# Hybrid attention and linear-recurrence block on one core: the seven-product output from token tile 2 on, weights' sums moved to VectorE in two rounds, the residual's loads moved

## The chip, the cores and the metric

One core of a Trainium2 chip. The metric is the device time in microseconds of one execution. TensorE (PE) multiplies, VectorE (DVE), ScalarE (ACT) and GpSimd (POOL) work elementwise, SyncE (SP) issues nearly all DMAs; ACT issues the stores of the result.

## The reference, cut to what matters

```python
h = rmsnorm(x, w_norm_pre)                      # x: 2048 x 1024, fp32
proj = h @ w_in                                 # 1024 x 3328
q_a, k_a, v_a, z_a, q_r, f_r, i_r, z_r = split(proj)
o_a = sliding_window_sink_attention(rope(q_a), rope(k_a), v_a, sinks) * silu(z_a)   # 8 heads of 64, chunks of 64, window 128
o_r = rmsnorm(hgrn2_chunkwise(q_r, f_r, i_r, lb), hgrn_norm) * silu(z_r)            # 4 heads of 128, a state carried along the sequence
y = concatenate([o_a, o_r]) @ w_out             # 1024 x 1024
x = x + rmsnorm(y, w_norm_post)
```

## The kernel before, in words

The sequence is cut into four token tiles (TILES, index t) of N = 512 tokens. All matmuls of the projections take fp32 operands split in two parts, a rounded one (hi) and the rest (lo); a product is hi x hi + hi x lo + lo x hi, so three matmuls for each block of 128 input features.

In each token tile PE first computes 26 products of the projection (w = 0 to 25: K, V, four tiles of Q, four of the attention's gate Z, then for each of the four recurrent heads forget, query, value and gate), 24 matmuls of 512 columns each, in `products` (line 566). Between them `between` places the small matmuls of attention (scores, transposes of the probabilities, their product with the values) and of the recurrence at fixed places (w, m). Then comes the output product. In token tile 0 it is plain (`out_plain`): eight weight tiles (OUT0 to OUT0 + 7), 192 matmuls (line 575) into eight PSUM banks. In token tiles 1 to 3 (t >= FAST, FAST = 1) it is done with seven products of half-sized blocks instead of eight (`out_fast`, line 822): four weight tiles of w_out as they are (B11, B21, B12, B22) and four sums of them (T1 to T4), against mixes that are also sums (s3, S1, S2, S4). It has 14 weight tiles P1A to P3B of 1 MB (hi and lo), each used by 12 matmuls, 168 in all, in the order UNITS.

Each engine runs its own queue in program order. The other engines go through steps s = 0 to 33 of a token tile; in step s they treat mainly product s - 1. DVE's steps 2 to 7 hold the turns of rope (`rope_turn`, lines 1288 to 1299), 7 to 10 the gates, 8 to 15 the softmax of four pairs of chunks (`softmax_first`, `softmax_sums`), 11 to 26 the heads' gates and scans, and after each head's output `gate_head`, `mix_head` and, in tiles with seven products, `sum_head`, which makes S2, S1 and S4 of the head. The queue's order is written out by hand.

Weights come through SP. In tile 0, and for the first six of tile 1 (index below FRESH), a raw tile of 0.5 MB is loaded into one of four slots of w_raw, ACT makes its hi part (`split_hi`), DVE its lo part (`split_lo`, line 1230), and SP saves both to DRAM (`save_split`); later tiles load the saved pair (`load_split`, line 449: 0.5 MB hi, 0.5 MB lo) into one of four slots of w_hi and w_lo. A slot is loaded when the product that used it last is done (`wait_slot`) and its save has landed (`wait_saved`, line 362). In each round of the loop over w, SP first may load a raw tile, then save, then load a pair, then issue loads of x for the next token tile (`load_x` at w = H0 + 0, 2, 4, 6), and so on; what stands first holds the rest.

T1 to T4 are made in tile 1, in two rounds (SUMS_AT = steps 5 and 11): SP loads the four quarters of w_out raw (`load_sums`, at w = 6 and 13), POOL forms four differences in w_raw (line 1653), ACT the four hi parts in mix_hi and mix_lo (`sums_high`, line 982), POOL the four lo parts (line 1658), SP saves all (`save_sums`, lines 467 and 468, at w = 11 and 18).

At the end of a token tile the output is scaled by the post norm's weights (`post`, L1425), its squares are summed on ACT (`square_fast`), and the result is y * scale + residual (`finish_y`, L1430, one DVE instruction for each 128x512 block; two of the eight blocks go to POOL in two instructions, L1706 and L1708). The residual is loaded into x_in by two DMAs of 1 MB (`load_residual`, line 485). In tiles with seven products they are issued after the loads of P3A and of P3B. After the last final, DVE makes the low part of the next tile's sum of squares (`x_low`, L1481), which PE wants before product 2 (`sum_x`).

Of the kernel before, what the change touches and what calls it, by code (L numbers as in the profile page):

```python
# [30 lines left out]
P = 128  # L31
# [30 lines left out]
FAST = 1  # L62
# [6 lines left out]
SPLIT_SLOT = SPLIT_SLOT + [w % 4 for w in range(FAST_WT)] * (TILES - FAST)  # L69
assert WT == 34 and OUT0 == 26 and FAST_WT % 4 == 0 and FAST == 1  # L70
# [8 lines left out]
def index(t, w):  # L79
    return w if t == 0 else WT + (t - FAST) * FAST_WT + w  # L80


def where(i):
    return (0, i) if i < WT else (FAST + (i - WT) // FAST_WT, (i - WT) % FAST_WT)
# [84 lines left out]
class Count:  # L169
# [4 lines left out]
    def __init__(self, sem, per_tile, first=None):  # L174
        self.sem, self.per_tile, self.first = sem, per_tile, per_tile if first is None else first
# [4 lines left out]
    def after(self, tile, i):  # L180

        assert -(self.first or self.per_tile if tile == 1 else self.per_tile) <= i < (self.per_tile if tile else self.first)
        return self.per_tile + (self.first + (tile - 1) * self.per_tile if tile else 0) + i + 1


def hybrid_block(nc, x, x_rows, weights, cos, sin, vectors, w_post, squares, out, kept):
# [3 lines left out]
    with ctx:  # L190
# [138 lines left out]
        y_read, y_biased, finished = count("y_read", 8), count("y_biased", 1), count("finished", 8 - len(Y_POOL))  # L329
# [545 lines left out]
        def _(act):  # L875
# [133 lines left out]
            for t in range(TILES):  # L1009
                links[0] = 0  # L1010
                for s in range(WT):
# [72 lines left out]
                    if t == FAST:  # L1084
                        for j, first in enumerate(SUMS_AT):
                            for k in (0, 1) if s == first + 2 else (2, 3) if s == first + 3 else ():
                                sums_high(4 * j + k)
# [682 lines left out]
```

## Time and profile before

| | us |
|---|---|
| median of three runs | 906.81 (905.63 to 908.21) |
| profiled execution | 907.85 |
| its span, first to last instruction | 906.0 |
| PE busy | 862.3 (95%) |
| DVE, ACT, POOL busy | 655.3, 525.8, 167.9 |

The profile is of one execution. Times in its views are microseconds from the span's start; what is added to the span for the execution's time is 1.85 us. PE is busy as long as a matmul is under way; since matmuls are pipelined, one of 512 columns is shown with 0.39 us while the next starts 0.227 us after it. SPq is SP's DMA issue. The clock is the one granted to TensorE as a share of 2.4 GHz.

### The profile page before, as it was taken

To read this page: it belongs to the slowest core of one execution; us is meant where nothing else is said; L and a number is where in the kernel's file an instruction comes from. 1 tells how busy PE (TensorE), PEld (TensorE's weight loads), DVE (VectorE), ACT (ScalarE), POOL (GpSimd) and SP (SyncE) were. 2 spreads that over 40 slices of the span, in tenths; PEclk is the share of its full clock that TensorE was granted. 3 is DMA by queue.
4 is the path that set the end of the run, shared out by engine and by line. 5 is a ranking of instruction groups with operands and counts; after the bars stand their busy time and mean duration, and the time that the engine had idled before them with its cause. 6 is when DMAs were issued, how large, how long until landed. Compare 5 with 4: busy or idle time off the path is not lost.

```text
span 906.0 us, 12482 instructions
## 1 busy us (share of the span) xinstructions
PE 862.3 (95%) x4406; PEld 703.4 (78%) x4406; DVE 655.3 (72%) x1127; ACT 525.8 (58%) x1041; POOL 167.9 (19%) x109
## 2 busy tenths in 40 slices
PE   7999999999998987999979999999989999999994
PEld 6887888888876776887868877888868887888883
DVE  6778868773775798889654579998755368987835
ACT  7666456563565457666535555865833755667533
POOL 0000014320244062252120000144202000013112
PEclk9999999999998998999999999999999999999998
DMA  8685755649877957455897554454789544443677
GB/s 308 219 308 193 280 209 181 231 154 410 349 254 289 392 228 298 169 181 192 300 377 289 205 193 163 140 183 166 277 331 367 197 174 146 166 153 143 226 282 279
DMA packets 61709, 217.49 MB, mean 240 GB/s; under 512 B 6864, under 2 KB 7120, under 8 KB 61648
## 3 DMA queue, kind: packets, MB, share of 16 engines
q1 hardware_dynamic: 58912, 209.75, 63.4%
q10 hardware_dynamic: 2736, 6.95, 1.9%
q8 instruction: 35, 0.57, 0.2%
q14 instruction: 26, 0.21, 0.1%
HBM read 164.25 MB, written 52.43 MB: 239 GB/s over the span
## 4 chain that ended last, share of the span: by engine, by line
PE 57%; DVE 20%; DMA 10%; ACT 5%; issue 4%; SPq 3%; POOL 1%; DVEq 0%; ACTq 0%
PE bank L566 41%; DMA w_lo<-kept_lo 4%; PE bank L822 3%; DVE kv_tok L1352 3%; DMA kept_lo<-w_lo 3%; PE turn_b L822 3%; PE score_b L822 2%; PE score_b L599 2%; ACT probs_t L923 1%; DVE q_gate L1430 1%; PE turn_b L623 1%; DMA x_in<-in_x_rows 1%; PE turn_b L676 1%; PE turn_b L679 1%; DVE f_c L1594 1%
## 5 line engine op out<-in xcount | busy, mean ns | idle before, releaser
L566 PE MATMUL bank<-h_hi,w_hi 128*128 128x512 f32 x832 | 326.5, 393 | 6.5 <-DMA w_lo<-kept_lo 4.8
L566 PE MATMUL bank<-h_hi,w_lo 128*128 128x512 f32 x832 | 329.0, 395 | 0.0
L566 PE MATMUL bank<-h_lo,w_hi 128*128 128x512 f32 x832 | 327.5, 394 | 0.0
L566 PEld LDWEIGHTS bank<-h_hi,w_hi 128*128 128x128 f32 x832 | 157.5, 189 | 40.7 <-DMA w_lo<-kept_lo 6.4
L566 PEld LDWEIGHTS bank<-h_lo,w_hi 128*128 128x128 f32 x832 | 157.3, 189 | 35.1 <-issue 3.3
L566 PEld LDWEIGHTS bank<-h_hi,w_lo 128*128 128x128 f32 x832 | 157.3, 189 | 33.2 <-issue 0.5
L1673 POOL TENSOR_TENSOR mix_lo<-v_r,mix_hi 128x512 fp32r<-128x512 f32 x16 | 21.2, 1325 | 424.1 <-ACT v_r L1111 424.1
L1230 DVE TENSOR_TENSOR w_lo<-w_raw,w_hi 128x1024 fp32r<-128x1024 f32 x37 | 45.8, 1248 | 33.4 <-ACT w_hi L896 32.9
L1352 DVE STREAM_TRANSPOSE kv_tok<-k_mid 32x128 f32<-32x128 f32 x192 | 58.1, 303 | 2.8
L896 ACT ACTIVATE w_hi<-w_raw 128x1024 fp32r<-128x1024 f32 x38 | 39.7, 1050 | 22.4 <-DMA kept_lo<-w_lo 9.0
L911 ACT ACTIVATE g_a<-g_a 128x512 f32<-128x512 f32 x32 | 20.2, 632 | 47.0 <-DVE g_a L1310 47.0
L900 ACT ACTIVATE g_a<-g_b 128x512 f32<-128x512 f32 x32 | 20.1, 629 | 44.3 <-DVE g_b L1306 44.3
L1643 POOL TENSOR_TENSOR x_acc<-x_acc,x_sq 128x512 f32<-128x512 f32 x21 | 30.0, 1427 | 75.7 <-ACT x_sq L946 75.7
L1430 DVE SCALAR_TENSOR_TENSOR q_gate<-q_gate,y_stats,x_in 128x512 f32<-128x512 f32 x24 | 27.3, 1172 | 18.4 <-DMA x_in<-in_x_rows 17.6
L1310 DVE SCALAR_TENSOR_TENSOR g_a<-g_b,g_a 128x512 f32<-128x512 f32 x32 | 24.9, 779 | 17.8 <-ACT g_a L902 17.8
L1036 ACT ACTIVATE f_b<-bank 32x512 f32<-32x512 f32 x48 | 28.3, 589 | 15.8 <-PE bank L566 15.2
L932 ACT ACTIVATE kv_tok<-f_d 32x128 f32<-32x128 f32 x96 | 29.5, 307 | 7.0 <-DVE f_d L1534 6.0
L1706 POOL TENSOR_TENSOR q_gate<-q_gate,y_stats 128x512 f32<-128x512 f32 x8 | 10.1, 1264 | 113.8 <-DMA x_in<-in_x_rows 81.4
L1653 POOL TENSOR_TENSOR w_raw<-w_raw 128x1024 f32<-128x1024 f32 x8 | 21.0, 2632 | 50.5 <-DMA w_raw<-in_weights 50.2
L932 ACT ACTIVATE probs<-f_d 32x128 f32<-32x128 f32 x96 | 29.5, 307 | 1.2
L1594 DVE TENSOR_TENSOR_SCAN f_c<-reset,f_b 128x512 f32<-128x512 f32 x16 | 19.6, 1225 | 11.5 <-ACT f_b L1094 11.5
L822 PE MATMUL score_b<-w_hi,s_hi 128*128 128x512 f32 x36 | 15.2, 423 | 12.7 <-DMA w_lo<-kept_lo 12.7
(265 smaller groups left out, 1657.6 us busy)
## 6 DMA issues: line engine op xcount, KB each, us to landing
w_hi<-kept_hi SPq DMA_DIRECT2D x114, 512.0 KB, 3.7
w_lo<-kept_lo SPq DMA_DIRECT2D x114, 512.0 KB, 4.7
w_raw<-in_weights SPq DMA_DIRECT2D x46, 512.0 KB, 5.8
kept_hi<-w_hi SPq DMA_DIRECT2D x34, 512.0 KB, 6.3
kept_lo<-w_lo SPq DMA_DIRECT2D x34, 512.0 KB, 7.2
x_in<-in_x_rows SPq DMA_DIRECT2D x8, 1024.0 KB, 10.3
x_in<-in_x SPq DMA_DIRECT2D x15, 512.0 KB, 6.7
out<-q_gate ACTq DMA_DIRECT2D x9, 512.0 KB, 7.9
```

The source lines that it names most:

```text
L566: mm = pe.matmul(acc(w)[:, :], stationary[:, s, k, :], moving[:, k, :], start=(m == 0), stop=(m == 3 * KT - 1), skip_group_check=True)
L822: mm = pe.matmul(into, mix, weight, start=w in (P1A, P7A, P2A, P4A) and k == 0 and part == 0, stop=k == KT // 2 - 1 and part == 2, skip_gr ...
L896: act.activation(w_hi[:, SPLIT_SLOT[i], :, :], w_raw[:, i % RAW_SLOTS, :, :], ACT.Copy).then_inc(hi_split.sem, 1)
L932: copy = act.activation(square(v_tok(t, h), j, i), square(f_d[:, :], i, j), ACT.Copy)
L1036: copy = act.activation(dst[32 * b:32 * b + 32, :], acc(s - 1)[32 * (b ^ 1):32 * (b ^ 1) + 32, :], ACT.Copy)
L1230: dve.tensor_tensor(w_lo[:, s, :, :], w_raw[:, i % RAW_SLOTS, :, :], w_hi[:, s, :, :], ALU.subtract).then_inc(lo_split.sem, 1)
L1310: dve.scalar_tensor_tensor(g_a[:, :], g_b[:, :], 0.0, g_a[:, :], ALU.min, ALU.subtract).then_inc(gate_arg.sem, 1)
L1352: last = dve.transpose(square(kv_tok[:, 0, :], j, i), square(k_mid[:, :], i, j))
L1430: dve.scalar_tensor_tensor(y, y, y_scale[:, b:b + 1], x_in[:, 2 * b + half, :], ALU.mult, ALU.add).then_inc(finished.sem, 1)
L1594: then(t, dve.tensor_tensor_scan(f_c[:, :], reset[:, :], f_b[:, :], 0.0, ALU.mult, ALU.add))
L1643: pool.tensor_tensor(x_acc[:, :], x_acc[:, :], x_sq[:, :], ALU.add).then_inc(x_added.sem, 1)
L1673: pool.tensor_tensor(o_sq_lo, o_sq[:, :], o_sq_hi, ALU.subtract).then_inc(o_low.sem, 1)
```

## The change

- FAST becomes 2: tile 1 is a plain tile too, with eight output products, its weights in slots as in tile 0. Seven products are used in tiles 2 and 3.
- The two rounds of the weights' sums are made in tiles 1 and 2, one in each, with SP's loads at w = 6 and saves at w = 12. The differences and low parts go from POOL to DVE (`sum_weights`), two instructions at the end of each of the steps 5 to 8; ACT's hi parts come at steps 6 and 7.
- UNITS: P2B, P6B, P4B one after the other, each with its k = 2 and 3, where k was the outer loop.
- The residual of a tile with seven products is loaded after the load of P3B, both halves; that of the last tile already at w = H0 and H0 + 1.
- `sum_head` of the first three heads, and the difference s3 before them, go to the end of DVE's step.
- All eight finals of a tile with seven products are made on DVE; the posts of the last two blocks stand before them (in the last tile beside them), and the order of stores follows.

```diff
-FAST = 1
+FAST = 2
...
-SPLIT_SLOT = SPLIT_SLOT + [w % 4 for w in range(FAST_WT)] * (TILES - FAST)
+SPLIT_SLOT = SPLIT_SLOT * FAST + [w % 4 for w in range(FAST_WT)] * (TILES - FAST)
...
-UNITS += [(w, k, i) for k in (2, 3) for w in (P2B, P6B, P4B) for i in range(2)]
+UNITS += [(w, k, i) for w in (P2B, P6B, P4B) for k in (2, 3) for i in range(2)]
...
-STORES = ((2, (0, 1), 1, 1), (3, (0,), 2, 0), (3, (1,), 3, 0), (0, (0, 1), 4, 2), (1, (0, 1), 6, 0))
-LAST_STORES = STORES[:-1] + ((1, (0,), 5, 0), (1, (1,), 6, 0))
+STORES = ((2, (0, 1), 2, 0), (3, (0,), 3, 0), (3, (1,), 4, 0), (0, (0, 1), 6, 0), (1, (0, 1), 8, 0))
+LAST_STORES = STORES[:-1] + ((1, (0,), 7, 0), (1, (1,), 8, 0))
...
-SUMS_IN, SUMS_OUT = (6, 13), (11, 18)
-SUMS_AT = (5, 11)
+SUMS_IN, SUMS_OUT = 6, 12
+SUMS_AT = 5
+RES_AT = ((WT - 3, WT - 1),) * FAST + ((P3B, P3B),) * (TILES - FAST - 1) + ((H0, H0 + 1),)
...
-                    if t == FAST and w in SUMS_IN:
-                        load_sums(SUMS_IN.index(w))
-                    if t == FAST and w in SUMS_OUT:
-                        save_sums(SUMS_OUT.index(w))
-                    if w == (P3A if t >= FAST else WT - 3):
+                    if FAST - 1 <= t <= FAST and w == SUMS_IN:
+                        load_sums(t - FAST + 1)
+                    if FAST - 1 <= t <= FAST and w == SUMS_OUT:
+                        save_sums(t - FAST + 1)
+                    if w == RES_AT[t][0]:
                         load_residual(t, 0)
-                    if w == tiles_of(t) - 1:
+                    if w == RES_AT[t][1]:
                         load_residual(t, 1)
...
+            def sum_weights(j, part):
+
+                raw = lambda r: w_raw[:, r, :, :]
+                if part < 2:
+                    dve.wait_ge(t_raw, 64 * (j + 1))
+                    for k, dst, a, b in ((0, 0, 2, 0), (1, 2, 3, 2)) if part == 0 else ((2, 3, 3, 0), (3, 1, 1, 3)):
+                        if k:
+                            dve.wait_ge(t_sum, 4 * j + k)
+                        dve.tensor_tensor(raw(dst), raw(a), raw(b), ALU.subtract).then_inc(t_sum, 1)
+                else:
+                    dve.wait_ge(t_sum, 4 * j + 4)
+                    for k, r in ((0, 0), (1, 2)) if part == 2 else ((2, 3), (3, 1)):
+                        dve.wait_ge(t_high, 4 * j + k + 1)
+                        dve.tensor_tensor(raw(r), raw(r), t_hi[r].rearrange("p k n -> p (k n)").rearrange("p (k m) -> p k m", m=P), ALU.subtract).then_inc(t_low, 1)
+
...
+            def post_last(t, i):
+
+                dve.wait_ge(y_squared.sem, y_squared.after(t, 6 + i))
+                post(t, 6 + i, x_bank[i], i, 1)
...
+                for i in range(2) if t + 1 < TILES else ():
+                    post_last(t, i)
                 dve.wait_ge(res_loaded, t * 32 + 32)
-                dve.wait_ge(y_posted.sem, y_posted.after(t, 5))
-                dve.wait_ge(y_rstd.sem, y_rstd.after(t, 0))
-                finish_y(t, 2, 1)
-                dve.wait_ge(y_rstd.sem, y_rstd.after(t, 1))
-                finish_y(t, 3, 0)
-                finish_y(t, 3, 1)
-                dve.wait_ge(y_squared.sem, y_squared.after(t, 6))
-                post(t, 6, x_bank[0], 0, 1)
-                dve.wait_ge(y_rstd.sem, y_rstd.after(t, 2))
-                dve.wait_ge(y_posted.sem, y_posted.after(t, 6))
-                finish_y(t, 0, 1)
-                dve.wait_ge(y_squared.sem, y_squared.after(t, 7))
-                post(t, 7, x_bank[1], 1, 1)
-                dve.wait_ge(y_rstd.sem, y_rstd.after(t, 3))
-                finish_y(t, 1, 0)
-                dve.wait_ge(y_posted.sem, y_posted.after(t, 7))
-                finish_y(t, 1, 1)
+                for i, b in enumerate((2, 3, 0, 1)):
+                    if t + 1 == TILES and b < 2:
+                        post_last(t, b)
+                    dve.wait_ge(y_rstd.sem, y_rstd.after(t, i))
+                    finish_y(t, b, 0)
+                    dve.wait_ge(y_posted.sem, y_posted.after(t, (6, 7, 4, 5)[b]))
+                    finish_y(t, b, 1)
...
                             mix_head(t, h)
-                            if t >= FAST:
+                            if t >= FAST and h == HEADS - 1:
                                 sum_head(t, h)
...
+                    if s == SCORES0 + 2 * PAIRS + 2 and t >= FAST:
+                        dve.wait_ge(gated.sem, gated.after(t, PAIRS - 1))
+                        dve.tensor_tensor(s3, a11, a21, ALU.subtract).then_inc(a_sum.sem, 1)
+                    for h in range(HEADS - 1):
+                        if s == out_step(h) + 2 and t >= FAST:
+                            dve.wait_ge(a_sum.sem, a_sum.after(t, 0))
+                            sum_head(t, h)
+                    if FAST - 1 <= t <= FAST and 0 <= s - SUMS_AT < 4:
+                        sum_weights(t - FAST + 1, s - SUMS_AT)
...
-                    if t == FAST and s in SUMS_AT:
-                        sum_weights(SUMS_AT.index(s))
...
-                for i, b in enumerate(Y_POOL if t < FAST else (2, 0)):
+                for b in Y_POOL:
```

## Rows read from the trace of the kernel before

**Rows 1.** The page: busy us (share of the span) and instructions of each engine.
```profile
PE 862.3 (95%) x4406; PEld 703.4 (78%) x4406; DVE 655.3 (72%) x1127; ACT 525.8 (58%) x1041; POOL 167.9 (19%) x109
```
**Rows 2.** Stretches: length, busy us of PE, PEld, DVE, ACT, POOL, clock, DMA share, GB/s.
```profile
181.80:228.70 46.90, 46.90 (x219) 39.23 (x218) 24.02 (x38) 23.41 (x39) 5.48 (x4) 1.00 0.73 287
228.70:292.50 63.80, 59.53 (x259) 47.91 (x258) 44.00 (x50) 39.29 (x78) 25.84 (x12) 0.95 0.79 290
292.50:417.00 124.50, 114.89 (x621) 93.10 (x620) 106.78 (x192) 74.89 (x157) 42.13 (x23) 0.96 0.65 245
417.00:466.50 49.50, 44.32 (x197) 35.85 (x197) 32.91 (x62) 27.66 (x62) 9.15 (x8) 0.97 0.86 316
466.50:522.70 56.20, 56.20 (x260) 46.35 (x259) 29.15 (x44) 29.53 (x59) 2.62 (x2) 1.00 0.73 262
522.70:634.80 112.10, 110.91 (x621) 90.46 (x620) 97.17 (x190) 70.22 (x152) 22.77 (x15) 1.00 0.47 166
634.80:684.10 49.30, 44.37 (x198) 35.68 (x196) 33.08 (x63) 27.66 (x62) 9.34 (x8) 0.97 0.86 317
```
**Rows 3.** PE's waits, total us, times, longest; and one in the timeline.
```profile
PE score_b L822 <- DMA w_lo<-kept_lo: 12.7, 6, 3.7
PE turn_b L623 <- ACT probs_t L923: 5.3, 2, 5.1
PE bank L667 <- DVE a_t L1324: 2.0, 3, 0.9
...
678.12 0.50 PE L822 MATMUL score_b<-w_hi,s_hi 128*128 128x512 f32 x1 [3.46 <-DMA w_lo<-kept_lo]
```
**Rows 4.** SP's waits from 240 to 300 us: total us, times, longest.
```profile
SPq L362 <- DMA kept_lo<-w_lo: 27.8, 4, 8.5
```
**Rows 5.** Sums and rope turns in the timeline (start, us); the page's group of line 1230.
```profile
259.78 10.79 POOL L1653 TENSOR_TENSOR w_raw<-w_raw 128x1024 f32<-128x1024 f32 x4 [24.12 <-DMA w_raw<-in_weights]
262.75 2.77 DVE L1299 TENSOR_TENSOR q_gate<-f_c,f_d 128x512 f32<-128x512 f32 x1
502.22 0.69 DVE L1292 TENSOR_TENSOR f_a<-bank,cos_t 128x512 f32<-128x512 f32 x1 [3.42 <-ACT f_b L1036]
503.54 0.69 DVE L1299 TENSOR_TENSOR q_gate<-f_a,f_b 128x512 f32<-128x512 f32 x1
...
L1230 DVE TENSOR_TENSOR w_lo<-w_raw,w_hi 128x1024 fp32r<-128x1024 f32 x37 | 45.8, 1248 | 33.4 <-ACT w_hi L896 32.9
```
**Rows 6.** Low parts of P5B (issued 664.33) and K (669.77), from issue to landing.
```profile
DMA to landing us min/median/max: 4.6/4.6/4.6
...
DMA to landing us min/median/max: 14.2/14.2/14.2
```
**Rows 7.** The chain of waits: start, us, matmuls in a row without a wait.
```profile
134.06 16.79 PE bank L566 x74
```
**Rows 8.** DVE's timeline around the output's start in tile 2.
```profile
639.36 0.68 DVE L1306 TENSOR_TENSOR g_b<-bank,x_scale 128x512 f32<-128x512 f32 x1
...
657.71 0.68 DVE L1519 TENSOR_TENSOR mix_lo<-h_mix,mix_hi 128x512 fp32r<-128x512 f32 x1
658.70 0.96 DVE L1522 TENSOR_TENSOR s_lo<-q_gate,s_hi 128x768 fp32r<-128x768 f32 x1 [0.31 <-ACT s_hi L1083]
```
**Rows 9.** Stretches of steps 5 to 8 and 9 to 12 in tile 2.
```profile
493.70:517.20 23.50, 23.50 (x115) 19.29 (x114) 10.41 (x16) 12.63 (x24) 0.00 (x0) 1.00 0.57 202
517.20:545.20 28.00, 28.00 (x178) 21.73 (x178) 21.87 (x34) 14.26 (x24) 0.00 (x0) 1.00 0.53 188
```
**Rows 10.** Stretches at the end of tile 2.
```profile
661.00:664.00 3.00, 3.00 (x14) 2.48 (x14) 0.02 (x1) 0.00 (x0) 0.00 (x0) 1.00 0.58 218
...
679.00:682.60 3.60, 3.60 (x11) 2.81 (x10) 1.93 (x2) 1.18 (x4) 1.81 (x2) 0.53 1.02 406
```
**Rows 11.** The end in the timeline.
```profile
895.17 4.75 DVE L1430 SCALAR_TENSOR_TENSOR q_gate<-q_gate,y_stats,x_in 128x512 f32<-128x512 f32 x3 [5.33 <-DMA x_in<-in_x_rows]
896.65 0.39 PE L822 MATMUL turn_b<-w_lo,s_hi 128*128 128x512 f32 x1
898.12 0.20 ACT L938 ACTIVATE y_stats<-y_stats 128x1 f32<-128x1 f32 x1
902.12 1.40 DVE L1430 SCALAR_TENSOR_TENSOR q_gate<-q_gate,y_stats,x_in 128x512 f32<-128x512 f32 x2
```

More of the change, by code:

```diff
@@ L79, in index @@
 def index(t, w):
[L80 removed]
+    return t * WT + w if t < FAST else FAST * WT + (t - FAST) * FAST_WT + w
 def where(i):
[L84 removed]
+    t, w = divmod(i, WT)
+    return (t, w) if t < FAST else (FAST + (i - FAST * WT) // FAST_WT, (i - FAST * WT) % FAST_WT)
 def tiles_of(t):
@@ L169, with __init__ @@
 class Count:
-    def __init__(self, sem, per_tile, first=None):
-        self.sem, self.per_tile, self.first = sem, per_tile, per_tile if first is None else first
+    def __init__(self, sem, per_tile, early=None):
+        early = per_tile if early is None else early
+        self.sem, self.sizes, self.per_tile = sem, [early] * FAST + [per_tile] * (TILES - FAST), max(early, per_tile)
     def start(self, engine):
@@ L180, in after @@
     def after(self, tile, i):
-        assert -(self.first or self.per_tile if tile == 1 else self.per_tile) <= i < (self.per_tile if tile else self.first)
-        return self.per_tile + (self.first + (tile - 1) * self.per_tile if tile else 0) + i + 1
+        assert -self.per_tile <= i < self.sizes[tile]
+        return self.per_tile + (sum(self.sizes[:tile]) if tile >= 0 else tile * self.per_tile) + i + 1
 def hybrid_block(nc, x, x_rows, weights, cos, sin, vectors, w_post, squares, out, kept):
@@ L328, in hybrid_block @@
         f_arg, f_d_scaled = count("f_arg", HEADS), count("f_d_scaled", HEADS)
-        y_read, y_biased, finished = count("y_read", 8), count("y_biased", 1), count("finished", 8 - len(Y_POOL))
+        y_read, y_biased, finished = count("y_read", 8), count("y_biased", 1), Count(sem("finished"), 8, 8 - len(Y_POOL))
         dve_step = count("dve_step", 1 + len(ROPE_TILES) + PAIRS * 5 + HEADS * 8)
@@ L1083, in _ @@
                             act.activation(s_hi[:, :, head, :], s_tmp, ACT.Copy).then_inc(s_high.sem, 1)
[L1084 to L1087, printed above, removed]
+                    if FAST - 1 <= t <= FAST and s in (SUMS_AT + 1, SUMS_AT + 2):
+                        for k in range(2):
+                            sums_high(4 * (t - FAST + 1) + 2 * (s - SUMS_AT - 1) + k)
                     for i in splits(t, s) if s > K_TILE + 1 or s + t == 0 else ():
@@ L1146, in _ @@
                         act.wait_ge(gated.sem, gated.after(t, PAIRS - 1))
+                        if t == FAST - 1 and j == 0:
+                            act.wait_ge(t_saved, 16 * T_TILES)
                         act.activation(mix_hi[:, j, :], q_gate[:, QT + j, :], ACT.Copy).then_inc(mixa_hi.sem, 1)
@@ L1559, in _ @@
                                           ALU.mult).then_inc(gated.sem, 1)
-                        if q == PAIRS and t >= FAST:
-                            dve.wait_ge(gated.sem, gated.after(t, PAIRS - 1))
-                            dve.tensor_tensor(s3, a11, a21, ALU.subtract).then_inc(a_sum.sem, 1)
                     for h in range(HEADS):
@@ L1643, in add_x @@
                 pool.tensor_tensor(x_acc[:, :], x_acc[:, :], x_sq[:, :], ALU.add).then_inc(x_added.sem, 1)
-            def sum_weights(j):
-                raw = lambda r: w_raw[:, r, :, :]
-                pool.wait_ge(t_raw, 64 * (j + 1))
-                for k, (dst, a, b) in enumerate(((0, 2, 0), (2, 3, 2), (3, 3, 0), (1, 1, 3))):
-                    if k > 1:
-                        pool.wait_ge(t_sum, 4 * j + k)
-                    pool.tensor_tensor(raw(dst), raw(a), raw(b), ALU.subtract).then_inc(t_sum, 1)
-                for k, r in enumerate((0, 2, 3, 1)):
-                    pool.wait_ge(t_high, 4 * j + k + 1)
-                    if k == 0:
-                        pool.wait_ge(t_sum, 4 * j + 4)
-                    pool.tensor_tensor(raw(r), raw(r), t_hi[r].rearrange("p k n -> p (k n)").rearrange("p (k m) -> p k m", m=P), ALU.subtract).then_inc(t_low, 1)
             pool.memset(carry[:, :, :], 0.0)
@@ L1697, in _ @@
                             split_lo(i)
-                if t < FAST:
-                    pool.wait_ge(y_read.sem, y_read.after(t, 3))
+                if t >= FAST:
+                    continue
+                pool.wait_ge(y_read.sem, y_read.after(t, 3))
                 pool.wait_ge(res_loaded, t * 32 + 32)
-                for i, b in enumerate(Y_POOL if t < FAST else (2, 0)):
+                for b in Y_POOL:
                     y = q_gate[:, 2 * b, :]
-                    pool.wait_ge(y_rstd.sem, y_rstd.after(t, b if t < FAST else 2 * i))
-                    if t >= FAST:
-                        pool.wait_ge(y_posted.sem, y_posted.after(t, b))
+                    pool.wait_ge(y_rstd.sem, y_rstd.after(t, b))
                     pool.tensor_tensor(y, y, y_scale[:, b:b + 1].broadcast_to([P, N]), ALU.mult).then_inc(y_scaled.sem, 1)
-                    pool.wait_ge(y_scaled.sem, y_scaled.after(t, i))
+                    pool.wait_ge(y_scaled.sem, y_scaled.after(t, b // 2))
                     pool.tensor_tensor(y, y, x_in[:, 2 * b, :], ALU.add).then_inc(finished_pool.sem, 1)
```

4 lines of the change are left out of this document (2 added, 2 removed).

## The prediction

> **What bounds the kernel now.** I read the page first. TensorE (PE) is busy 95% of the span [rows 1]; what can be gained is therefore in PE's waits, in matmuls that disappear, and in the tail. Next the stretches [rows 2], cut where the products of the projection (line 566) end and the output's begin. They say how the four token tiles differ. Tile 1 runs from 228.7 to 466.5 = 237.8 us, tile 2 from there to 684.1 = 217.6. Tile 1's first ten projection products take 63.8 us against 56.2 in tile 2, its other sixteen 124.5 against 112.1. Its output with seven products takes 49.5 (tile 2: 49.3); tile 0's output with eight takes only 46.9, at clock 1.00 and with PE busy all through.
>
> The waits of PE, summed and singly [rows 3], tell why: 12.7 us for the last weights of the seven-product outputs, six times, at most 3.7; once 5.1 us for ACT, in tile 1; DVE costs it 2.0 us in the head steps.
>
> Three causes stand behind them. (a) In tile 1 SP waits four times, 27.8 us in all, for a store of split weights to land before it may load the next tile into the same slot [rows 4]. That is 7 us a time and more than the 5.4 us of a product, so it makes the loss of the first ten products. (b) POOL's sums of weights, all in tile 1: the first four instructions take 10.79 us, and three more such groups follow [rows 5]. While they run, a rope operation on DVE takes 2.77 us; its like in tile 2 takes 0.69. That and SP's stores behind POOL make the loss of the other sixteen. (c) At an output's end SP issues the last weights in between two residual loads of 1 MB.
>
> **The change, part by part.** *Tile 1 becomes a plain tile.* Eight products are 192 matmuls for 168. One costs 16.79/74 = 0.227 us [rows 7], 24 cost 5.4. But the plain output has 5.4 us for each 1 MB of weights where the other has 2.7, so its end waits for no DMA. Hence I take tile 0's 46.9 for it, plus 1.1: its fourth bank is first written some 4 us in, and DVE frees it at 639.36, 4.6 us after the output's start in tile 2 (634.8), behind transposes that tile 0 doesn't have [rows 8]. So 48.0, bounds 46.9 (tile 0) and 54.9 (49.5 + 5.4).
>
> *The first ten products of tile 1* keep cause (a): the saves, their slots and the raw loads of the first sum round stay where they are. 63.8 again; bounds 56.2 and 67.
>
> *The weights' sums, on DVE in two rounds.* A round is four subtractions and four low parts of 128x1024, in the form that takes DVE 1.25 us (line 1230) [rows 5]: 10 us, in tile 1 and again in tile 2, at the ends of steps 5 to 8. In the same steps of tile 2 DVE is busy 10.4 of 23.5 us [rows 9], idle 13.1. The first four instructions fall into gaps like the 3.42 us before the rope turn of 502.22 [rows 5]. The last four fall on the gates and the first softmax, where gaps are shorter; DVE comes out of step 8 some 3 us late, and has 28.0 - 21.9 = 6.1 us idle in the next stretch to make it good, while PE runs up to three banks ahead of it. I cost a round at 1.0; bounds 0 (all in gaps) and 10 (all on PE's path). ACT has four copies in a round, in a stretch with 23.5 - 12.6 = 10.9 us idle: nothing. SP's saves (8 issues, 4 MB) stand behind the load of product 12, and what queues behind them is the load of product 13. At the 0.4 MB a us of 679.0 to 682.6 [rows 10] the saves and that load need some 14 us from product 8's end; product 13 begins 28 us after it [rows 9]: nothing. Without that cover PE would wait for weights as at each output's end, 3.5 us.
>
> With POOL's sums gone from products 10 to 25 of tile 1, these take tile 2's 112.1, plus 1.0 for the round = 113.1; bounds 112.1 and 124.5. Tile 1: 63.8 + 113.1 + 48.0 = 224.9, **12.9 less**.
>
> *A tile's end.* Of the twelve units in the middle of the output P2B's now come first, so its slot is free after four units, not eight, and the load of P5B starts 2.7 us sooner, P3A's 1.4. What the new order needs sooner is ready: the fourth head's low parts are written from 657.7 to 659.7 [rows 8], the second pair of P2B's units starts near 659.8. The residual goes behind P3B. Before, P5B landed at 664.3 + 4.6 = 668.9, P3B released PE at 678.1 [rows 3], and K, the next tile's first weight, issued at 669.8, landed 14.2 us later, at 684.0 [rows 6]. That last one is the point: tile 3 starts at 684.1, so K is late as well and hides behind P3B's wait. Moving the residual brings P3B forward, not K; P5B's earlier issue does. From 661 to 664 the DMA engines were busy 0.58 [rows 10]; that gap and its sequel are some 2.6 us. With transfers that follow each other at 2.6 us per MB: P5B 666.5, P3A 669.2, P3B 671.8 (needed 673.3), residual 677, K 680.0. PE is through with P3 at 671.9 + 24 x 0.227 = 677.4 and waits 2.6 us for K. So tile 3 starts 4.1 us sooner. But after the 3.46 us wait at 678.12 the clock falls to half (0.53 in 679.0 to 682.6, 11 matmuls in 3.6 us) [rows 10], 1.4 us lost, and that now falls on K's product. Net 2.7; bounds 0 (K lands as before) and 6.7 (684.1 - 677.4). Tile 2: 1.0 - 2.7, **1.7 less**. Tile 1 has no such end.
>
> By the page "TensorE: Matmul & The Clock Gate" of the Trainium skill, § HAM oscillation, waits for a DMA between bursts of matmuls let the clock fall, and a shorter wait may leave it up. The row shows the fall behind 3.46 us; with a clock that holds at 2.6 us the sum would be 1.4 lower.
>
> *The last tile.* Its residual is loaded at product 10, in a stretch whose DMA share is 0.47 in tile 2 [rows 2]: nothing. So no 2 MB stand among its last weights, whose waits of 0.6 + 0.3 + 3.5 and the gaps around them end: the last matmul starts at 891.5, where it is 896.65 [rows 11] (P2B's first unit at 872.6, then 84 matmuls of 0.227 less one). From there square and scale took 898.32 - 896.65 = 1.7 us; then two finals. One takes DVE 0.7 us alone (1.40 for two), 1.6 beside POOL (4.75 for three) [rows 11]. So 893.2, with the post 893.4, finals 894.9, the last store 2.2 with its issue: 897.1, where the end is 906.0. **8.9 less**; bounds 6.2 (finals at 1.6, P3B 0.9 late) and 9.6 (one final left behind the scale).
>
> *Finals on DVE* in tile 2: eight of 0.7 = 5.6 us after the residual and the posts: 684.5. PE wants the statistic that DVE makes next at 680 + 11.4: nothing; if the residual lands 6 us late it begins to cost. ACT's stores stand before its work on K (686.5): nothing.
>
> *A head's sums at the step's end*: the same instructions behind others; PE's waits for DVE there are 0.9 us at most, 2.0 in all [rows 3]. Nothing taken; bounds -1.5 and +1.
>
> **Sum** against the profiled execution (907.85 us, span 906.0, so 1.85 around it): -12.9 - 1.7 - 8.9 = -23.5, span 882.5, execution 884.4. That execution lies 1.04 above the median of the three runs, 906.81; so I predict **883.3 us**.
>
> **Rivals.** (1) *The late part of tile 1 is not POOL's doing*, but comes from the transfers that stay in it (saves, 2 MB in, 4 MB out). For: DMA 0.65 there against 0.47 [rows 2]. Against: DVE's operations stretch while POOL works [rows 5]. The 124.5 would stay: 883.3 + 11.4 = 894.7. Chance 0.10.
> (2) *Slower: DVE becomes the bound.* In steps 8 to 17 each softmax and head operation waits for the one before it on DVE. If the 3 us that the sums leave over meet no gap, DVE's queue, not POOL, makes tile 1's sixteen products late (124.5 stays) and both rounds lie on the path (2 x 10 instead of 2): 883.3 + 11.4 + 18 = 912.7. It decides once DVE's idle time behind step 8 (6.1 us) is less than what it brings along. Chance 0.04. With half of that the time is about 898: 0.05.
> (3) *K gains nothing.* If the transfers share instead of following each other, P3B lands near 676 and not 671.8, and K stays at 684: 2.7 more in tile 2, 1 in the last tile: 887. Against it: K's 14.2 us are just the transfers issued ahead of it. Chance 0.10. The page "DMA: Bandwidth & Descriptors" of the Trainium skill, § Two DMAs through the same engine are not ordered, says as much: to be issued first is not to be finished first.
> (4) *Still better*: the saves in tile 1 land sooner, or the clock holds and K comes in time: 4 (6.7 - 2.7) to 8 less, near 877. Chance 0.10.
>
> **Numbers.** Forecast 883.3, own range 879 to 888, chance 0.60; the rest as above, with 0.01 for a change that doesn't do what it says. The range of eight in ten: 877 to 893. A difference of 0.3% (2.7 us) is about what a measurement of this kernel tells from none. Faster by more than that 0.94, within it 0.02, slower 0.04.
>
> **What would show it.** Tile 1: 64 us for ten products with SP's waits for the stores still there, 113 for sixteen with no rope operation over 1 us, output 48 with no DMA wait. Tile 2: no wait inside P3, one of 1 to 4 us before the first product of tile 3, released by K. Tile 3: last matmul about 5 us nearer to the last product of the projection, no DVE wait for the residual, end 5.6 us after the last matmul's start. Wrong it would be if DVE's operations of steps 8 to 17 ran late (PE waiting at lines 613, 623 or 599), or if K's wait took all that P3 gave.

## The result, and the profile after

The kernel after takes 884.62 us in the median (880.8 to 885.51, four executions), beside 906.22 of the kernel before: ratio 0.9752, 95% interval 0.9718 to 0.9786. That is 21.6 us less; 883.3 was predicted. The profiled execution is the fastest of the four: 880.8 us, span 879.0. It gained twice by chance. Tile 0's first product took 7.9 us where the trace before shows 10.4: before, the granted clock was 0.50 from 10.2 to 13.6 us, after it was 1.00 there. And a product behind a wait ran at full clock (below).

First the page's row of busy time; it answers to [rows 1].

```profile
PE 855.7 (97%) x4430; PEld 701.4 (80%) x4430; DVE 635.3 (72%) x1125; ACT 520.4 (59%) x1033; POOL 114.6 (13%) x84
```

PE has 24 matmuls more and is busy 6.6 us less: what went are waits and stretches at the lower clock. Next the stretches, cut and laid out as in [rows 2]: tile 1's first ten products, its other sixteen, its output; the same three of tile 2; tile 3's projection; its output with the tail.

```profile
226.40:290.20 63.80, 58.62 (x260) 47.17 (x260) 45.69 (x58) 40.08 (x79) 5.75 (x4) 0.97 0.80 293
290.20:400.40 110.20, 110.20 (x622) 90.38 (x621) 90.92 (x187) 69.77 (x153) 21.04 (x15) 1.00 0.59 219
400.40:447.60 47.20, 47.20 (x222) 39.42 (x221) 22.12 (x45) 22.59 (x54) 6.47 (x6) 1.00 0.56 201
447.60:503.80 56.20, 56.20 (x260) 46.35 (x259) 37.52 (x50) 32.85 (x63) 3.39 (x3) 1.00 0.80 293
503.80:617.30 113.50, 111.17 (x621) 90.35 (x620) 96.31 (x192) 71.07 (x153) 24.04 (x15) 1.00 0.55 203
617.30:663.30 46.00, 42.12 (x197) 34.71 (x195) 33.10 (x65) 29.31 (x67) 6.02 (x5) 1.00 0.90 339
663.30:831.10 167.80, 166.40 (x872) 136.14 (x873) 120.03 (x228) 94.63 (x199) 14.77 (x9) 1.00 0.54 196
831.10:879.00 47.90, 41.78 (x195) 34.50 (x194) 29.22 (x58) 23.52 (x57) 4.72 (x4) 0.98 0.78 285
```

| part | before | predicted | after |
|---|---|---|---|
| to the end of tile 0 | 228.7 | 228.7 | 226.4 |
| tile 1: ten products, sixteen, output | 63.8 + 124.5 + 49.5 | 63.8 + 113.1 + 48.0 | 63.8 + 110.2 + 47.2 |
| tile 2: ten, sixteen, output | 56.2 + 112.1 + 49.3 | 215.9 in all | 56.2 + 113.5 + 46.0 |
| tile 3: projection, output and tail | 166.1 + 55.8 | 213.0 in all | 167.8 + 47.9 |

Then PE's waits, total us, times, longest; and the longest of them in the timeline. They answer to [rows 3].

```profile
PE bank L569 <- DMA w_lo<-kept_lo: 7.7, 3, 3.4
...
PE bank L660 <- issue: 2.1, 3, 0.8
PE turn_b L679 <- DVE read_state L1342: 1.1, 2, 0.6
...
663.30 0.50 PE L569 MATMUL bank<-h_hi,w_hi 128*128 128x512 f32 x1 [3.35 <-DMA w_lo<-kept_lo]
```

No wait for weights is left inside an output (line 825 is absent), nor the 5.1 us for ACT. Three waits for weights remain, all before a product: two in tile 1's first ten, one for K at tile 3's start. New is a wait for `read_state`.

### The profile page after: what moved, and what is told of

It reads as the page before. It is cut to its first block, busy times and chain, and to the rows that moved or that the text cites. A ratio compares the mean times of both kernels' runs of the same rounds, so it can differ in the third digit from the quotient of the medians.

```text
span 879.0 us, 12449 instructions
## 1 busy us (share of the span) xinstructions
PE 855.7 (97%) x4430; PEld 701.4 (80%) x4430; DVE 635.3 (72%) x1125; ACT 520.4 (59%) x1033; POOL 114.6 (13%) x84
## 4 chain that ended last, share of the span: by engine, by line
PE 64%; DVE 16%; ACT 8%; DMA 6%; issue 4%; SPq 1%; POOL 0%; DVEq 0%; ACTq 0%
PE bank L569 44%; DMA kept_lo<-w_lo 3%; PE bank L825 2%; PE bank L578 2%; PE turn_b L825 2%; PE score_b L825 2%; DVE kv_tok L1356 2%; DMA w_lo<-kept_lo 2%; PE score_b L602 2%; PE turn_b L626 1%; PE turn_b L578 1%; PE score_b L578 1%; DVE q_gate L1449 1%; PE turn_b L679 1%; PE bank L670 1%
## 5 line engine op out<-in xcount | busy, mean ns | idle before, releaser
L899 ACT ACTIVATE w_hi<-w_raw 128x1024 fp32r<-128x1024 f32 x38 | 39.8, 1051 | 22.9 <-issue 10.3
L1665 POOL TENSOR_TENSOR x_acc<-x_acc,x_sq 128x512 f32<-128x512 f32 x21 | 32.7, 1558 | 72.8 <-ACT x_sq L949 72.8
L1224 DVE SCALAR_TENSOR_TENSOR h_lo<-x_in,vec,h_hi 128x512 fp32r<-128x512 f32 x32 | 23.3, 774 | 3.5 <-ACT h_hi L953 3.5
L578 PE MATMUL bank<-w_hi,mix_lo 128*128 128x512 f32 x64 | 25.3, 395 | 0.0
L578 PE MATMUL bank<-w_hi,mix_hi 128*128 128x512 f32 x64 | 24.9, 389 | 0.0
L578 PE MATMUL bank<-w_lo,mix_hi 128*128 128x512 f32 x64 | 24.9, 389 | 0.0
```

Source lines behind the costliest of these rows:

```text
L578: mm = pe.matmul(y_bank[half][b][:, :], mix[:, k, b * P:(b + 1) * P], weight[:, SPLIT_SLOT[index(t, w)], (k % 2) * 4:(k % 2) * 4 + 4, :].r ...
L899: act.activation(w_hi[:, SPLIT_SLOT[i], :, :], w_raw[:, i % RAW_SLOTS, :, :], ACT.Copy).then_inc(hi_split.sem, 1)
L1224: dve.scalar_tensor_tensor(h_lo[:, k, :], x_in[:, k, :], w_pre[:, k:k + 1], h_hi[:, k, :], ALU.mult, ALU.subtract).then_inc(h_lo_done.sem, 1)
L1665: pool.tensor_tensor(x_acc[:, :], x_acc[:, :], x_sq[:, :], ALU.add).then_inc(x_added.sem, 1)
```

## The experiments

Ratios are to the kernel before; the kernel after has 0.9752. Each has an interval of about 0.0025 either side, some 2.3 us, that of the kernel after 0.0034, some 3 us. So a difference of 2 or 3 us between two kernels rests on their traces. Differences in us are those of the medians where nothing else is said; each group of runs had its own runs of the kernel before (medians of 905.3 to 906.7), so what a ratio says can differ from that by up to 2 us.

**A head's sums back where they were.**

```diff
-                            if t >= FAST and h == HEADS - 1:
+                            if t >= FAST:
                                 sum_head(t, h)
```

with the two blocks at the step's end taken out and s3 made behind the gates again.

> The changed kernel with s3 and the first three heads' sums back at their old place in DVE's step, right behind mix_head. Theory (the move costs: the third head's three sums, 1.0 us, now stand directly ahead of the state's carry, for which PE's head_out waits; product 25 of tiles 2 and 3 took 10.0 and 9.8 us where it took 8.6 and 8.2): product 25 back to 8.2 to 8.6, PE's waits at read_state (1.1 us in all) gone, 2.5 to 3.0 us less in all. Rival (it was the chance place of a POOL instruction beside DVE's): product 25 stays near 9.8, time within 1 us of the changed kernel.

Measured: 881.39 us, 0.9725 (0.9699 to 0.9751). The `read_state` waits are gone. Tile 2's sixteen products take 112.3 instead of 113.5; in tile 3 product 25 takes 8.1 instead of 9.8. That is 2.9 us for the move, which was priced at nothing. First DVE's and POOL's timeline after, ahead of product 25 of tile 3, and the PE instruction that waits:

```profile
821.43 0.42 DVE L1418 TENSOR_TENSOR q_gate<-h_mix,q_gate 128x256 f32<-128x256 f32 x1
821.76 0.42 DVE L1419 TENSOR_TENSOR q_gate<-h_mix,q_gate 128x256 f32<-128x256 f32 x1
822.10 0.42 DVE L1421 TENSOR_TENSOR q_gate<-h_mix,q_gate 128x256 f32<-128x256 f32 x1
...
823.53 2.08 DVE L1342 TENSOR_SCALAR read_state<-probs,to_next 128x128 f32<-128x128 f32 x2
...
823.71 1.82 POOL L1700 TENSOR_TENSOR s_lo<-q_gate,s_hi 128x768 fp32r<-128x768 f32 x1 [5.34 <-ACT s_hi L1086]
...
825.67 0.49 PE L679 MATMUL turn_b<-a_t,kv_tok 128*128 128x128 f32 x2 [0.56 <-DVE read_state L1342]
```

and the same pair with the sums back:

```profile
824.52 0.48 DVE L1342 TENSOR_SCALAR read_state<-probs,to_next 128x128 f32<-128x128 f32 x2
...
825.70 2.21 POOL L1696 TENSOR_TENSOR s_lo<-q_gate,s_hi 128x768 fp32r<-128x768 f32 x1 [5.33 <-ACT s_hi L1086]
```

The three sums cost 1.0 us themselves, straight ahead of the carry that PE wants. And the delay lets the `read_state` pair meet POOL's low part: it takes 2.08 us instead of 0.48 and ends at 825.61, just when POOL's 1.82 us are over (825.53). The page "SBUF — State Buffer" of the Trainium skill, § SBUF: two separate sides, says that DVE and GpSimd share a pair of ports, and that the one which takes it first holds it for its whole instruction while the other blocks; on DVE's side this goes for an instruction in a mode with two ports or with two inputs in SBUF. By that rule the second of the pair waits for POOL; the trace agrees: it starts at 823.72, 0.01 behind POOL's, and takes 1.89 where the first took 0.28.

**Which part of the old sums was dear: the engine, or the place?** Three kernels. The first round stays at tile 1's step 5; the second starts at tile 2's step 5 or 11, on POOL or DVE. Where it says POOL, both rounds run there, each eight instructions in a row, with ACT's hi parts one step later. With step 11 SP's loads and saves of the round move too:

```diff
-SUMS_IN, SUMS_OUT = 6, 12
-SUMS_AT = 5
+SUMS_IN, SUMS_OUT = (6, 13), (12, 18)
+SUMS_AT = (5, 11)
```

> The changed kernel with the weights' sums on POOL again, but in its own places: a round at step 5 of tile 1 and one at step 5 of tile 2. Theory A (the engine made the loss: POOL's sums stretch DVE's operations): rope turns of 2 to 3 us, products 10 to 25 of tile 1 or 2 longer by 5 us or more, 6 to 12 us slower than the changed kernel. Theory B (the place made it: at step 5 DVE has idle time, at step 11 it has none): rope turns stretched just as much, but no more than 1 us lost in each tile, within 2 us of the changed kernel.

> The changed kernel with DVE's second round at steps 11 to 14 of tile 2 instead of 5 to 8 (raw loads at w = 13, saves at w = 18). If DVE is the bound of the softmax steps, its 10 us there lie on PE's path: products 10 to 25 of tile 2 take 118 to 124 us for 113.5, PE waits at lines 616, 626 or 602, 5 to 10 us slower. If DVE has slack there too: within 1.5 us.

> As e3_dve_11, but both rounds on POOL: the first at step 5 of tile 1, the second at step 11 of tile 2, the places of the kernel before, one tile apart. Theory (the loss of 12 to 14 us in tile 1 before was this second round's): products 10 to 25 of tile 2 take some 125 us, 11 to 13 us slower than the changed kernel. Rival (the loss came from two rounds in one tile, that is from 12 MB of transfers): less than 5 us.

| second round | us | ratio | tile 2's sixteen products |
|---|---|---|---|
| DVE, step 5 (after) | 884.62 | 0.9752 | 113.5 |
| POOL, step 5 | 884.5 | 0.9766 (0.9741 to 0.9791) | 116.4 |
| DVE, step 11 | 890.84 | 0.9834 (0.9808 to 0.9859) | 122.8 |
| POOL, step 11 | 895.96 | 0.9891 (0.9869 to 0.9912) | 126.6 |

POOL at step 11 costs 13.1 us over the kernel after in this stretch; the stretch of the kernel before lost 12.4 to its tile 2 [rows 2]. So the old loss is made again, in another tile. Of the 13.1, 3.8 go with the engine and 9.3 remain with DVE at the same steps: the place is most of it. POOL's low part holds DVE as above. In the timeline of POOL at step 5, DVE's L1388, which takes 0.17 us the other 15 times, takes 2.14:

```profile
493.48 2.39 POOL L1678 TENSOR_TENSOR w_raw<-w_raw,mix_lo 128x1024 f32<-128x1024 f32 x1
...
493.76 2.14 DVE L1388 TENSOR_TENSOR s_stats<-s_stats,sink 128x8 f32<-128x8 f32 x1
495.93 0.17 DVE L1389 TENSOR_TENSOR s_stats<-sink,s_stats 128x8 f32<-128x8 f32 x1
```

At steps 5 to 8 that costs 2.9 us in tile 2 (116.4 for 113.5) and nothing in tile 1 (110.2 in both). So neither theory of that run holds in full: the time is as the place said, but tile 2 loses more than the 1 us that it allowed. At steps 11 to 14 either engine is dear; there the softmax and the first head follow each other on DVE, two low parts stand ahead of the next head's first operation and of the softmax, and PE waits for the probabilities. It waits for no DMA in these products, so SP's loads and saves, which moved too, are not the loss. The timelines with DVE at step 11, DVE's and PE's:

```profile
547.78 1.22 DVE L1436 TENSOR_TENSOR w_raw<-w_raw,mix_lo 128x1024 f32<-128x1024 f32 x1
548.92 1.22 DVE L1436 TENSOR_TENSOR w_raw<-w_raw,mix_hi 128x1024 f32<-128x1024 f32 x1
550.05 0.68 DVE L1517 TENSOR_TENSOR f_b<-bank,x_scale 128x512 f32<-128x512 f32 x1
...
564.91 1.98 PE L626 MATMUL turn_b<-probs_t,v_win 128*64 128x256 f32 x8 [4.70 <-ACT probs_t L926]
```

**The units' order undone** (k outside, as before).

```diff
-UNITS += [(w, k, i) for w in (P2B, P6B, P4B) for k in (2, 3) for i in range(2)]
+UNITS += [(w, k, i) for k in (2, 3) for w in (P2B, P6B, P4B) for i in range(2)]
```

> The changed kernel with the twelve middle units in the old order (k outside, P2B, P6B, P4B inside); the residual still behind P3B. Theory (P5B's earlier load is what brings K forward): P5B, P3A, P3B and K land 2 to 3 us later, PE waits inside P3 or longer before K, 2 to 3 us slower. Rival (the place of the residual made the gain, the order of the units none): within 1 us.

Measured: 887.12 us, 0.9797 (0.9775 to 0.9819), slower than after by 2.5 us in the medians and 4 by the ratios. Tile 2's output takes 49.1 (619.0 to 668.1), 3.1 more; in tile 3 the last matmul starts 43.7 behind the output's first, 2.3 more. PE waits inside the outputs for weights again:

```profile
PE score_b L825 <- DMA w_lo<-kept_lo: 2.9, 4, 1.2
```

K is later too: PE waits 4.02 for it, after 3.35. The order of the units carries the tile's end.

**Tile 2's residual in between, as before, and the last tile's residual late.** In the first `RES_AT` has (P3A, P3B) for tile 2, in the second for tile 3.

> The changed kernel with tile 2's residual issued as before, half behind P3A and half behind P3B; the last tile's stays early. Theory (K is the wall: it stands behind all of these transfers either way): PE waits inside P3 instead of before K, tile 3 starts within 0.5 us of where it did, time within 1 us. Rival (moving the residual made the gain): 3 to 4 us slower.

> The changed kernel with the last tile's residual at its old place, behind P3A and P3B. Theory: the wait inside the last P3 is back, the residual lands some 3 us before today's place of it, end 5 to 7 us later. If only DVE's finals had set the end: 2 us or less.

The middle one: 881.68 us, 0.9738 (0.9714 to 0.9762), not slower than after. The timeline:

```profile
657.72 0.50 PE L825 MATMUL score_b<-w_hi,s_hi 128*128 128x512 f32 x1 [2.02 <-DMA w_lo<-kept_lo]
...
664.22 0.50 PE L569 MATMUL bank<-h_hi,w_hi 128*128 128x512 f32 x1 [0.48 <-DMA w_lo<-kept_lo]
```

PE waits 2.02 for P3B, and then 0.48 for K where it otherwise waits 3.35 for K alone. The tile's output takes 47.1 (617.1 to 664.2) for 46.0. This 1.1 is less than the 1.6 that a fall of the clock costs (below), and here it falls inside P3:

```profile
657.70:661.90 4.20, 4.18 (x11) 3.32 (x12) 0.69 (x1) 1.19 (x4) 0.00 (x0) 0.59 1.02 414
```

K is the wall; the residual behind P3B only moves the wait to it.

The last tile's: 886.56 us, 0.9794 (0.9769 to 0.9819). PE waits 1.50 inside P3, the last matmul starts 43.2 behind the output's first instead of 41.4, and the end is 7.5 behind it instead of 6.5, since DVE's finals wait 2.8 for the residual: 2.8 us in all. 5 to 7 were expected. So the residual is the smaller part of what the last output gained, 5.1 up to its last matmul (46.5 to 41.4): 1.8 of it, and 2.3 are the units' order above, each undone alone; the last 1.0 neither shows by itself.

```profile
873.18 0.50 PE L825 MATMUL score_b<-w_hi,s_hi 128*128 128x512 f32 x1 [1.50 <-DMA w_lo<-kept_lo]
```

**Two finals back on POOL** (its code, counts and stores as before).

> The changed kernel with the old finals: two of eight blocks on POOL in two instructions each, DVE's others among the posts. With the last tile's residual early, these finals lie before the last matmul, and what is left behind it is DVE's one post and two finals: theory, within 0.7 us of the changed kernel. Rival (POOL's instructions stretch DVE's finals at the end): 2 to 4 us slower.

Measured: 883.53 us, 0.9767 (0.9742 to 0.9791): no difference that the ratios can show. In its trace the end is 8.2 us behind the last matmul's start (873.0 to 881.2), after 6.5; 1.7 us is what the finals on DVE brought in this one execution, more than the 0.7 that was expected: DVE's finals take 1.4 to 1.8 each beside POOL's, and the last posts stand behind them. In tile 2 they bring nothing: that tile takes 215.7 us (446.8 to 662.5), as after.

**Tile 2's residual behind K's load and ahead of V's** (`RES_AT` has (None, None) for tile 2).

```diff
+                    if w == 0 and t and RES_AT[t - 1][0] is None:
+                        load_residual(t - 1, 0)
+                        load_residual(t - 1, 1)
```

> The changed kernel with tile 2's residual issued behind the load of K of tile 3 (ahead of V). Theory (K waits only for what is issued ahead of it): K lands some 5 us sooner, before P3 ends; the 3.35 us wait and the slow clock on K's product go; the residual lands 2.6 us later than now, DVE's finals end near tile 3's start + 9 us, still ahead of product 2: 3 to 5 us less than the changed kernel. Rival (what the wait gives up comes back one step later, before V or before the sum of squares at product 2): the same sum of waits there, within 1 us.

Measured: 879.46 us, 0.9699 (0.9677 to 0.9722), 5.2 us less than after. K's wait is gone, tile 2's output takes 42.5 (619.4 to 661.9) for 46.0, and the clock stays at 1.00 behind it. In the traces tiles 2 and 3 are 3.3 us shorter than after. K's parts are issued 34.5 us behind the output's first matmul in both. From issue to landing, first both parts after (issued at 651.8 and 652.2; the low one took 11.1), then the low part alone here (issued at 654.2):

```profile
DMA to landing us min/median/max: 9.3/10.2/11.1
```

```profile
DMA to landing us min/median/max: 4.9/4.9/4.9
```

The 2 MB of the residual ahead of K were the wait.

**The saves of tile 1's first weights issued earlier**, each as soon as its parts can be made and not behind the next loads.

```diff
-                    if LATE + RAW_SLOTS <= i < FRESH + RAW_SLOTS:
+                    if LATE + RAW_SLOTS <= i <= FRESH:
                         save_split(i - RAW_SLOTS)
+                    if i == FRESH:
+                        save_split(i - 3)
+                        save_split(i - 2)
```

and the last one behind that round's loads.

> The changed kernel with the saves of tile 1's split weights 3 to 5 issued as soon as they are made (two before the load of product 6, one behind the raw loads) instead of one before each of the loads 7, 8 and 9. Theory (the chain save, landing, load, in SP's order, makes the loss of the first ten products): SP's waits for stores fall from 28 us to under 10, waits of 1.1 and 3.3 us before products 7 and 8 go, first ten products 56 to 58 us instead of 63.8, 5 to 7 us less. Rival (DMA bandwidth makes the loss): less than 2 us.

Measured: 878.32 us, 0.9685 (0.9663 to 0.9707), 6.3 less. Tile 1's first ten products take 56.3 for 63.8; product 10 then takes 10.4 for 8.5, with waits of 0.3 and, for ACT's probabilities, 1.3. SP's waits for the saves, from 240 to 300 us:

```profile
SPq L365 <- DMA kept_lo<-w_lo: 6.2, 2, 5.5
```

The transfers are the same as after, so the DMA engines' bandwidth did not make the loss.

**These three together**: sums of a head back, residual behind K, saves early.

> The changed kernel with three edits together: the heads' sums at their old place (2.9 us less alone), the residual behind K (3 to 5 expected) and the early saves (5 to 7 expected). If the three are independent: 11 to 15 us less than the changed kernel, some 870. If they share one slack: less than 9.

Measured: 870.56 us, 0.9605 (0.9582 to 0.9628); the parts alone had given 3.2 + 5.2 + 6.3 = 14.7, together 14.1. A little comes back at V, whose load is behind the residual: PE waits 0.7 us for it. It is the fastest kernel of this study. Tile 1's first ten products, its other sixteen, and tile 2's output:

```profile
226.10:282.90 56.80, 56.51 (x259) 46.23 (x258) 44.04 (x55) 38.57 (x77) 5.74 (x4) 1.00 0.93 351
282.90:394.30 111.40, 110.22 (x621) 90.39 (x620) 92.12 (x190) 70.48 (x155) 21.02 (x15) 1.00 0.55 205
...
610.00:652.50 42.50, 41.95 (x198) 34.89 (x197) 30.52 (x61) 27.47 (x62) 5.95 (x5) 1.00 0.90 333
```

**FAST = 3**: tile 2 plain as well, the rounds of sums in tiles 2 and 3, seven products in tile 3 only.

```diff
-FAST = 2
+FAST = 3
```

> The changed kernel with tile 2 plain as well, so that only the last tile has seven products (the sums' rounds in tiles 2 and 3). Tells what seven products bring in a middle tile. By matmuls alone it would be 5.4 us slower. Theory (a seven-product tile gives most of it back in the wait for K, the slower clock and the heads' sums ahead of the carry): a plain output of 47.2 us for one of 46.0 with its waits, product 25 shorter by 1.5, K's product by 1.6: between 1 us faster and 3 us slower.

Measured: 874.22 us, 0.9641 (0.9619 to 0.9662), 10.4 less than after. That was not expected. Its stretches: tile 1's first ten products, then tile 2's sixteen and its output.

```profile
228.40:285.30 56.90, 56.52 (x260) 46.27 (x259) 37.82 (x52) 36.38 (x75) 5.73 (x4) 1.00 0.80 291
...
498.80:609.40 110.60, 110.40 (x621) 90.45 (x620) 91.08 (x187) 69.50 (x153) 20.93 (x15) 1.00 0.56 208
609.40:656.70 47.30, 47.30 (x222) 39.41 (x222) 22.19 (x45) 22.61 (x54) 6.55 (x6) 1.00 0.57 201
```

Tile 2's output has 24 matmuls more (5.4 us) and takes only 1.3 longer, since the wait for K is gone; without a head's sums its sixteen products take 2.9 less. And tile 1's first ten, in which nothing of the output changes, take 6.9 less. What left that stretch is the first round: its raw loads, and DVE's and ACT's work on them. All of that is still there with the saves early, where the loss is gone as well, so it is the place of the raw loads in SP's queue that counts. First SP's waits for the saves, then its timeline, after: the raw load, and the hi parts of the load ahead of it and of the three behind it;

```profile
SPq L365 <- DMA kept_lo<-w_lo: 28.2, 4, 8.9
...
244.50 0.32 SPq L452 DMA_DIRECT2D w_hi<-kept_hi  x1
...
248.84 1.76 SPq L462 DMA_DIRECT2D w_raw<-in_weights  x4
...
260.82 0.32 SPq L452 DMA_DIRECT2D w_hi<-kept_hi  x1
...
269.90 0.32 SPq L452 DMA_DIRECT2D w_hi<-kept_hi  x1
...
278.94 0.32 SPq L452 DMA_DIRECT2D w_hi<-kept_hi  x1
```

and with FAST = 3:

```profile
SPq L365 <- DMA kept_lo<-w_lo: 27.4, 4, 7.9
...
246.06 0.32 SPq L452 DMA_DIRECT2D w_hi<-kept_hi  x1
...
255.03 0.32 SPq L452 DMA_DIRECT2D w_hi<-kept_hi  x1
...
264.75 0.32 SPq L452 DMA_DIRECT2D w_hi<-kept_hi  x1
...
273.80 0.32 SPq L452 DMA_DIRECT2D w_hi<-kept_hi  x1
```

SP waits for the same four saves, 27.4 us against 28.2, and PE waits for no weights. The waits for saves alone are covered. The raw load stands between a load and the next save. Tile 1 starts at 226.4 in the kernel after and at 228.4 with FAST = 3. Counted from there, the first load comes 0.4 us later in the kernel after, and the three behind the raw load come 7.8, 7.1 and 7.1 later. Of that SP waits 3.5 until DVE has made the low parts that it reads from w_raw, and issuing the raw load takes 1.8. That brings the chain out from under the products.

## Why the prediction was right, and where it was off

**Right: the sum and its signs, by errors that cancel.** -23.5 us was forecast for the spans. The profiled ones differ by 27.0, of which 2.3 is tile 0 (chance); the medians by 21.6. The parts were not all so near: tile 1 came out 3.7 us better than computed (221.2 for 224.9) and tile 3 2.7 worse (215.7 for 213.0). That the total fits to 1.3 us is in part luck.

**Right: tile 1 as a plain tile.** The first ten products take the predicted 63.8, the output 47.2 (48.0) without a wait for weights, and the rope turns are back at 0.69 us.

**Right: the chain at tile 2's end.** P5B and P3 come sooner by the order of the units (with the old order 3.1 us are lost), no wait is left inside P3, and K is the wall: 3.35 us where 2.6 was computed. The tile takes 215.7, predicted 215.9; that this is so near is luck. The 215.9 holds 1.4 for the slow clock, which did not come in this execution; in its place stand 0.8 more of output (46.0 for the 45.2 that 4.1 less than 49.3 makes) and 0.4 more in the sixteen products, where the heads' sums (+1.2, priced at nothing) ate what the round did not cost.

**Off: a round of sums, 1.0 us.** It costs 0.5 at most. In tile 2 its instructions run from 475.6 to 501.0, inside the first ten products, and these take 56.2 with the round as without [rows 2]. Behind it sixteen products of a plain tile without a round take 110.1 (tile 1 with FAST = 3, 285.3 to 395.4), with one 110.2 (after) or 110.6 (tile 2 with FAST = 3). And tile 2's 112.1 [rows 2] was the wrong base for tile 1, because the sums of the heads are in it; a plain tile has none. So tile 1 gained 2.9 more than the 113.1 said, and 0.8 more in its output.

**Off: a head's sums at the step's end, "nothing taken; bounds -1.5 and +1".** The step looked at PE's waits for DVE as they were, 2.0 in all [rows 3], and not at what would now stand behind the sums. Measured: +1.2 in tile 2, +1.7 in tile 3. In tile 3 the sums put 1.0 us ahead of the pair that PE wants, and push it into POOL's instruction, which adds 1.6; part of both is covered.

**Off: the last tile, 6.2 us gained and not 8.9.** The output up to its last matmul is as computed: 41.4 (41.3). But the sum laid all of that to the residual, and the experiments give it only 1.8 of the 5.1; the order of the units gives 2.3. The heads' sums cost 1.7. The tail is 6.5 and not 5.6. Its rows, which answer to [rows 11]:

```profile
869.92 2.73 DVE L1449 SCALAR_TENSOR_TENSOR q_gate<-q_gate,y_stats,x_in 128x512 f32<-128x512 f32 x4
...
872.50 0.39 PE L825 MATMUL turn_b<-w_lo,s_hi 128*128 128x512 f32 x1
...
873.17 1.41 DVE L1449 SCALAR_TENSOR_TENSOR q_gate<-q_gate,y_stats,x_in 128x512 f32<-128x512 f32 x2
874.49 0.69 DVE L1444 TENSOR_TENSOR q_gate<-turn_b,w_post_t 128x512 f32<-128x512 f32 x1
875.09 1.41 DVE L1449 SCALAR_TENSOR_TENSOR q_gate<-q_gate,y_stats,x_in 128x512 f32<-128x512 f32 x2
```

Finals alone do take 0.7 each (2.73 for four, 1.41 for two), as said; but the post begins only 2.0 behind the last matmul's start, since two finals of the block before (873.17) stand ahead of it on DVE; the finals end 2.0 later, and the store takes 2.5.

**Half right: causes (a) and (b).** (a) put the first ten products' loss on the waits for saves; they stay in full with FAST = 3 and the loss is gone. It takes both, the saves late in SP's queue and the raw loads between: with either one taken away the loss is gone (56.3 and 56.9 for 63.8). (b) put the sixteen products' loss on POOL; at the same place DVE loses 9.3 of POOL's 13.1. Both gave right numbers because the change left the one alone and moved the other in engine and place at once.

**The clock behind K's wait** was counted at 1.4. It holds in some executions and falls in others. The product behind the wait, in the kernel after (wait 3.35) and in that with early saves (wait 3.63); the clock is the third figure from the right:

```profile
663.30:668.90 5.60, 5.59 (x25) 4.63 (x26) 4.00 (x7) 0.00 (x0) 0.00 (x0) 1.00 1.03 389
```

```profile
659.80:667.00 7.20, 7.20 (x25) 5.78 (x26) 3.71 (x6) 0.00 (x0) 0.00 (x0) 0.76 1.02 380
```

The fall costs 1.6 us. Nine of the traces have a wait of 2.8 us or more before that product. In seven the clock fell, behind waits of 2.87 (last residual late), 3.24, 3.33, 3.44, 3.63, 4.02 and 4.47; in two it held, behind 3.31 (POOL at step 5) and 3.35 (after). So the length of the wait alone does not decide; what does is open. So the profiled execution of the kernel after was a lucky one. With tile 0's 2.3 us the fall makes 3.9, the distance of the profiled execution to the others' 884.6 (3.8). Of these others there is no trace, only the mean clock, 0.994 to 0.995 where the profiled one has 0.997; so that is argued, not shown.

**The rivals.** (1), that tile 1's late loss stays, fell: 110.2. (2), DVE as the bound, fell at steps 5 to 8; it is what happens at steps 11 to 14, where a round on DVE costs 9.3. (3), K gains nothing, fell: K landed 11.1 us after its issue, not 14.2. The residual's halves, issued at 649.9 and 650.4, landed after 7.2 and 10.3, at 657.1 and 660.7, K's low part at 663.3: here the transfers landed in the order of their issue. (4) was not needed in the change, but early saves and the residual behind K show that those gains were there (6.3 and 5.2).

**Missed: that seven products, as the change has them, are not worth it in tile 2.** They save 5.4 us of matmuls; the wait for K with the gaps around it (4.1) and the heads' sums (2.9) take more than that. The first can be removed and the second cut (tile 2's sixteen products take 112.4 in the combined kernel, 1.8 over FAST = 3): that kernel keeps seven products in tiles 2 and 3, and its median is 3.7 us below that of FAST = 3, though their intervals touch. Seven products in tile 3 alone together with early saves, and nothing else, was not tried.

## What to carry to other kernels

What an instruction costs on an engine's queue is set by what stands behind it: read the rows that follow in its new place, up to the one that PE waits for, and what the neighbouring engine does at that time. A wait in an issuing queue is harmless until something pushes the chain behind it past its cover, so price the chain, not the wait. And a stage with fewer matmuls must be charged for all that it needs: its weights come twice as fast, and its operands are made by an engine that has other work.

## What was not expected of the hardware

- A DVE pair of 128x128 instructions took 2.08 us beside a POOL instruction and 0.48 without; one on 128x8 took 2.14 for 0.17 (POOL at step 5).
- After a wait of PE of 3.35 us the granted clock stayed at 2.4 GHz (1.00 over the next product), after one of 2.87, with the last residual late, it fell to 1.2 GHz for a while (0.76).
- The low part of K's load, issued 2.7 us behind P3B's in both kernels, landed after 4.9 us without the residual's 2 MB ahead of it and after 11.1 with them.
